# Two one-column Exp instructions that load ScalarE's Exp table ahead of the two attention stages

## The reference

```
layer 0: x = x + gate * ([window attention(q, k, v) || retention(q, k, v)] @ w_out)
         x = x + gate * swiglu(modulate(rmsnorm(x)))
layer 1: x = x + gate * (neighbourhood attention(q, k, v) @ w_out)
         x = x + gate * moe(modulate(rmsnorm(x)))          # top 2 of 8 experts
attention:  p = exp(s - max(s)) / sum(...);   rmsnorm: x * rsqrt(mean(x*x) + eps)
```

## Time and profile before

| | |
|---|---|
| median of 3 runs | 2131.32 us (2129.88 to 2134.2) |
| the profiled execution: its own time, its span | 2135.14 us, 2133.4 us |
| busy over the span | PE 90%, PEld 69%, DVE 58%, ACT 51%, POOL 8% |
| mean granted clock of TensorE | 0.883 of full speed |
| granted clock from 888 to 1029 us (`attention(1)`) | 0.50 |
| `ACT_TABLE_LOAD` | 17 of 1283 ns each in the whole execution |

### The profile page before, as it was taken

One profiled execution on the slowest core, in us unless ns is written; L12 is line 12 of the kernel. 1 busy time (PEld: TensorE's weight loads), 2 busy tenths in 40 slices (PEclk: granted clock), 3 DMA queues, 4 the chain that ended last, 5 costly groups with the idle time before them and its releaser, 6 DMA issues.

```text
span 2133.4 us, 26695 instructions
## 1 busy us (share of the span) xinstructions
PE 1928.6 (90%) x9633; PEld 1470.7 (69%) x9634; DVE 1234.5 (58%) x1475; ACT 1082.9 (51%) x1482; POOL 162.5 (8%) x262
## 2 busy tenths in 40 slices
PE   4778899989999989999979999999899998989891
PEld 3456677768888868766767666657777676767671
DVE  3754645553433252333444655658878787878784
ACT  3755633433333233433324545558677777767771
POOL 3010000021000050141001000000000000000001
PEclk9979985589999989855858999999999999999996
DMA  8947640049444444210127777779999999999982
GB/s 274 333 160 223 216 136 10 1 124 332 128 126 122 121 125 137 82 30 31 41 79 219 237 234 238 228 241 352 336 320 334 322 330 326 339 324 322 324 309 102
DMA packets 204805, 440.90 MB, mean 207 GB/s; under 512 B 16648, under 2 KB 36160, under 8 KB 204672
## 3 DMA queue, kind: packets, MB, share of 16 engines
q1 hardware_dynamic: 188928, 394.31, 55.5%
q0 software_dynamic: 15744, 44.73, 6.6%
HBM read 413.69 MB, written 25.30 MB: 206 GB/s over the span
## 4 chain that ended last, share of the span: by engine, by line
PE 79%; DVE 9%; ACT 6%; issue 3%; DMA 2%; POOL 0%; SPq 0%; ACTq 0%; DVEq 0%; POOLq 0%
PE ps L511 21%; PE ps L512 19%; PE ps L513 19%; PE ps L949 4%; PE ps L981 3%; PE ps L1199 2%; PE ps L959 2%; DVE wlo L484 2%; ACT whi L480 2%; DMA rawb<-in_mod_w 2%; ACT whi L456 2%; DVE wlo L461 2%; PE ps L1217 1%; PE ps L1162 1%; DVE h L1728 1%
## 5 line engine op out<-in xcount | busy, mean ns | idle before, releaser
L461 DVE TENSOR_TENSOR wlo<-rawb,whi 128x1024 fp32r<-128x1024 f32 x224 | 270.9, 1229 | 346.9 <-ACT whi L456 345.7
L484 DVE TENSOR_TENSOR wlo<-rawb,whi 128x1024 fp32r<-128x1024 f32 x288 | 347.9, 1223 | 166.2 <-ACT whi L480 164.4
L456 ACT ACTIVATE whi<-rawb 128x1024 fp32r<-128x1024 f32 x224 | 232.0, 1055 | 353.8 <-PE ps L513 320.0
L480 ACT ACTIVATE whi<-rawb 128x1024 fp32r<-128x1024 f32 x288 | 303.9, 1061 | 154.0 <-PE ps L513 78.2
L511 PE MATMUL ps<-whi,eT_hi 128*128 128x512 f32 (+1 forms) x768 | 312.7, 407 | 36.2 <-issue 27.0
L484 DVE TENSOR_TENSOR wlo<-rawx,whi 128x1024 fp32r<-128x1024 f32 x240 | 289.5, 1223 | 90.0 <-ACT whi L480 88.7
L480 ACT ACTIVATE whi<-rawx 128x1024 fp32r<-128x1024 f32 x240 | 252.6, 1061 | 109.7 <-PE ps L513 52.7
L512 PE MATMUL ps<-wlo,eT_hi 128*128 128x512 f32 (+1 forms) x768 | 295.1, 384 | 0.0
L513 PE MATMUL ps<-whi,eT_lo 128*128 128x512 f32 (+1 forms) x768 | 293.3, 382 | 0.0
L511 PE MATMUL ps<-whi,hT_hi 128*128 128x512 f32 (+1 forms) x672 | 261.2, 389 | 20.0 <-DVE wlo L461 17.0
L512 PE MATMUL ps<-wlo,hT_hi 128*128 128x512 f32 (+1 forms) x672 | 257.1, 383 | 0.0
(11 more groups left out here) (296 smaller groups left out, 2404.4 us busy)
## 6 DMA issues: line engine op xcount, KB each, us to landing
rawb<-in_od_moe_w_gu SPq DMA_DIRECT2D x192, 512.0 KB, 5.6
rawx<-in_od_moe_w_gu SPq DMA_DIRECT2D x160, 512.0 KB, 5.7
rawb<-in_mod_w SPq DMA_DIRECT2D x96, 512.0 KB, 5.3
rawb<-in_od_moe_w_down SPq DMA_DIRECT2D x96, 512.0 KB, 5.1
rawx<-in_od_moe_w_down SPq DMA_DIRECT2D x80, 512.0 KB, 4.8
rawb<-in_ev_ffn_w_gu SPq DMA_DIRECT2D x44, 512.0 KB, 3.7
rawb<-in_od_w_qkv SPq DMA_DIRECT2D x24, 512.0 KB, 3.7
rawb<-in_ev_w_in SPq DMA_DIRECT2D x22, 512.0 KB, 3.7
```

Of the source, the lines that this page charges most:

```text
L456: nc.scalar.activation(whi[:, r, :], rawb[:, s, :], ACT.Copy).then_inc(hi_done, 1)
L461: nc.vector.tensor_tensor(wlo[:, r, :], rawb[:, s, :], whi[:, r, :].bitcast(F32), ALU.subtract).then_inc(lo_done, 1)
L480: nc.scalar.activation(whi[:, moe_slot(i), :], moe_raw(j), ACT.Copy).then_inc(hi_done, 1)
L484: nc.vector.tensor_tensor(wlo[:, moe_slot(i), :], moe_raw(i % EB), whi[:, moe_slot(i), :].bitcast(F32), ALU.subtract).then_inc(lo_done, 1)
```

## The change

Two activations are added to ScalarE's program, one at the end of `retention()` behind its three Silu, one behind `norm(2, 3)` ahead of the layer 1 projection. Each takes Exp of a constant column that is written once at the start of the kernel and writes one column that nothing reads. Neither waits for a semaphore nor signals one. Nothing else in the program is changed; where the compiler puts its table loads follows from it.

```diff
@@ retention() on ScalarE
                 for t in range(T):
                     nc.scalar.activation(proj0[:, t, O_GR:], proj0[:, t, O_GR:], ACT.Silu).then_inc(gn_a, 1)
+                nc.scalar.activation(first[:, 10:11], first[:, 5:6], ACT.Exp)
@@ ScalarE's main sequence
             split_rows(2)
             ahead.to(B_QKV + HL)
             norm(2, 3)
+            nc.scalar.activation(first[:, 11:12], first[:, 5:6], ACT.Exp)
             dense(QKV_CH, GM_DONE[1], proj1, lambda c: prep(1, 0) if c == len(QKV_CH) - 2 else None)
             attention(1)
```

## The result

The changed kernel took 2068.17 us (median of 4, 2060.8 to 2128.51) against 2130.6 us (2128.16 to 2134.2) for the kernel before on the same chip. The forecast was 2128.9. The profiled execution took 2060.8 us, with a span of 2059.0 and a mean granted clock of 0.921 (0.883 before).

What follows compares the result with a forecast made beforehand. The prediction took TensorE to hold most of the chain and ScalarE little. Its terms, 0 + 0 + 0 - 2.4 us, took the median from 2131.3 to 2128.9 us, range 2125.8 to 2132.8.

Steps and rivals of the forecast that it cites:

- Start of attention(0), and the two new Exp: Table load ahead of attention(0)'s first Exp lies in idle time, both new Exp are covered: 0 us each.
- Start of attention(1): Table load lies on the path; without it the first Exp comes 1.29 to 1.38 us earlier, taken as 1.33.
- What the clock makes of it: In attention(1) the clock's fall stays put, so 1.33 us more work at the higher clock saves 2.4 us.
- Rival C: At attention(1)'s start the closed gap holds the clock up longer: 4.8 us saved in all, 2126.5 us; chance 0.14.
- To the end: From 888 to 1029 TensorE is busy at clock 0.50, so the lead is kept through attention and expert stage.
- rival B: Later clock edges in the expert stage take the gain back: 2130.5 to 2132.1 us, middle 2131.3; chance 0.17.
- D: Rival: a load stands again ahead of attention(1)'s first Exp, the change does nothing: 2131.3 us; chance 0.04.
- E: Rival: slower, each added clock fall in the expert stage costs 1.6 us: 2136.9 us from the fifth; chance 0.03.

Runs made afterwards that it cites:

- first Exp alone: The changed kernel with only the new Exp behind the Silu of retention(), without the one behind norm(2, 3): 2125.34 to 2141.24 us in twelve executions, ratio 1.0008.
- burst in attention(0): The changed kernel with 24 float32r products of 384 columns added at unit 0 of attention(0): 2130.8 to 2146.87 us in twelve executions, ratio 1.0033.
- stand of 1.48 us: The changed kernel with 12 one-column Exp ahead of the first Exp of attention(1): 2128.09 to 2138.91 us in twelve executions, ratio 0.9997.
- before, gap filled: The kernel before with 11 unread TensorE products ahead of attention(1)'s first transpose, table load kept: 2070.31 to 2075.3 us in three executions, 2128.94 to 2136.74 in four.

## Why the prediction was wrong

*Start of attention(0), and the two new Exp:* right. 0 us for all three, shown by the first Exp alone (1.0008) and by the idle times.

*Start of attention(1):* right as far as it goes. The load was on the path and the stand shrank from 1.81 to 0.38 us, for an expected 0.48. What the page "ScalarE: Activation LUTs" of the Trainium skill, section "What ACT_TABLE_LOAD costs", says of some 1380 ns of drain beside the load still shows nowhere here: the new load starts at 323.48, 0.02 us behind the Silu, and its Exp 0.02 us behind the load.

*What the clock makes of it: the step that failed.* "So I take it that the fall belongs to the end of the projection, whose time the change doesn't move, and stays where it is." The fall keeps no distance from the projection: it came 2.7 us behind the last projection product (first Exp alone), 2.8 (burst in attention(0)), 5.2 (before, and with the stand of 1.48 us), 9.6 (changed kernel, the lost execution) and 12 (before, gap filled), and in the profiled execution of the changed kernel not at all within the attention. It hung on the stand that the change shortens. With a stand of 1.48 us the clock fell in 12 of 12 executions, with 0.38 in 2 of 9, and with it filled and the load in place it could be kept. The stand isn't the whole of it, as the burst in attention(0) shows. The term was put at 2.4 us and is about 62, because the sum moved the fall by nothing and a kept clock is worth the whole attention.

*Rival C had the right mechanism and the wrong size.* It let the clock hold some 5 us longer, by the retention's case of 10.3 us, and gave 4.8 us and a chance of 0.14. It took for granted that small products lose the clock sooner or later, because they had in the earlier trace rows at 303.2 to 306.6. The attention's products need not: at 1.00 they held it for 80 us in the profiled execution of the changed kernel, and at 0.50 they didn't raise it in 141 us of nearly unbroken work. The rows of before had only the second half of that. The sentence "from 888 to 1029 the clock stays at 0.50", read as a property of the stage, was a property of what happened in its first microseconds.

*To the end, and rival B:* the executions of one kernel in one group differ by 10 to 20 us, so an edge more or less can't be told. It didn't decide anything. *D and E* did not occur.

*Open:* why the changed kernel still loses the clock in 2 of 9 executions, with the same stands in both of its traces; why a burst in attention(0) loses attention(1) in twelve of twelve with a stand of 0.38 us; and why the retention's unbroken products lose the clock, and the attention's don't. I tried nothing for the last. For the second I know only that the fall then comes by 889 us, 3 us behind the last projection product at 886.2.

## What to carry to other kernels

A stage that runs at the low TensorE clock from its first microseconds to its end should be asked how it began. Price a wait at the head of such a stage by the whole stage at the other clock: here 1.3 us of ScalarE stood for 62 us. Look for every stretch early in the stage in which other engines make TensorE wait, shorten it or fill it, and count executions, since such a kernel has two times and a median of few can show either. A stand at the head is the first suspect, not the only one: here the clock also fell behind later stands of 0.7 us.

## What the runs showed that I had not expected

The same products have two lasting levels: 147.7 / 48 = 3.1 us a unit nearly all at 0.50, and 82.9 / 48 = 1.7 at 1.00, and executions of one and the same kernel end up at either. A burst of 24 products, 6.96 us long, was enough to change over for the 73 us of attention that followed. And useless work can pay: 11 products that nothing reads made the kernel before 60 us faster in three of seven executions.
